# First units of a two-block transformer kernel: order of the first norm, idle products, weights in halves, gates in PSUM

## What is computed

```python
u = rmsnorm(h, norm_mix[layer])             # x * rsqrt(mean(x*x) + eps) * gain
proj = u @ w_in                             # q, f, i, g
forget = lb + (1.0 - lb) * jax.nn.sigmoid(f)
key = 1.0 - forget
log_f = jnp.log(forget)
query = jax.nn.silu(q)
# chunkwise: b = cumsum(log_f); decays exp(b_t - b_s) between query t and key s
```

## Time and profile before

| | |
|---|---|
| time, median of 3 runs | 2152.67 us (2152.38 to 2156.83) |
| the profiled execution's own time | 2158.04 us |
| its span | 2156.2 us |
| busy: PE, DVE, ACT, POOL | 2120.2, 995.1, 868.8, 1149.7 us |
| mean granted TensorE clock | 0.995 of full |

### The profile page before, as it was taken

One profiled execution on the slowest core, in us unless ns is written; L12 is line 12 of the kernel. 1 busy time (PEld: TensorE's weight loads), 2 busy tenths in 40 slices (PEclk: granted clock), 3 DMA queues, 4 the chain that ended last, 5 costly groups with the idle time before them and its releaser, 6 DMA issues. The chain is left out here.

```text
span 2156.2 us, 28081 instructions
## 1 busy us (share of the span) xinstructions
PE 2120.2 (98%) x10271; PEld 1750.4 (81%) x10271; DVE 995.1 (46%) x1562; ACT 868.8 (40%) x1250; POOL 1149.7 (53%) x642
## 2 busy tenths in 40 slices
PE   7999999999999999999999999999999999999998
PEld 6788878888888988888888888888667888888886
DVE  6666564403442057745422436563783344422433
ACT  7677653312233234434322334453764234322323
POOL 5677755545554465455554565473224555554552
PEclk9999999999999999999999999999999999999999
DMA  6122133322332322133332332322102223332332
GB/s 214 59 68 68 59 97 94 107 93 88 97 108 80 96 88 69 57 105 98 97 106 89 98 106 89 120 72 89 69 21 79 97 89 98 97 108 85 94 112 70
DMA packets 54423, 195.65 MB, mean 91 GB/s; under 512 B 6832, under 2 KB 9664, under 8 KB 53952
## 3 DMA queue, kind: packets, MB, share of 16 engines
q1 hardware_dynamic: 52864, 187.27, 27.7%
q10 hardware_dynamic: 1472, 7.19, 0.9%
HBM read 190.25 MB, written 4.19 MB: 90 GB/s over the span
## 5 line engine op out<-in xcount | busy, mean ns | idle before, releaser
L1764 POOL TENSOR_TENSOR w_split<-ring,w_split 128x1024 fp32r<-128x1024 f32 (+3 forms) x327 | 841.3, 2573 | 827.1 <-ACT w_split L1237 827.0
L1237 ACT CAST w_split<-ring 128x1024 fp32r<-128x1024 f32 (+3 forms) x327 | 356.4, 1090 | 1007.6 <-PE ps L498 876.1
L496 PE MATMUL ps<-u_split,w_split 128*128 128x512 f32 x1768 | 705.5, 399 | 10.5 <-DVE u_split L2019 9.8
L498 PE MATMUL ps<-u_split,w_split 128*128 128x512 f32 x1768 | 691.0, 391 | 0.0
L497 PE MATMUL ps<-u_split,w_split 128*128 128x512 f32 x1768 | 690.8, 391 | 0.0
L496 PEld LDWEIGHTS ps<-u_split,w_split 128*128 128x128 f32 x1768 | 333.6, 189 | 87.6 <-issue 16.9
L498 PEld LDWEIGHTS ps<-u_split,w_split 128*128 128x128 f32 x1768 | 333.2, 188 | 70.5
L497 PEld LDWEIGHTS ps<-u_split,w_split 128*128 128x128 f32 x1768 | 333.8, 189 | 69.6 <-issue 3.1
L496 PE MATMUL ps<-hid,w_split 128*128 128x512 f32 x637 | 249.0, 391 | 1.5 <-POOL hid L1959 1.4
L498 PE MATMUL ps<-hid,w_split 128*128 128x512 f32 x637 | 247.9, 389 | 0.0
L497 PE MATMUL ps<-hid,w_split 128*128 128x512 f32 x637 | 247.9, 389 | 0.0
(11 more groups left out here) (355 smaller groups left out, 2511.1 us busy)
## 6 DMA issues: line engine op xcount, KB each, us to landing
ring<-in_w_hgrn SPq DMA_DIRECT2D x32, 512.0 KB, 3.6
ring<-in_w_attn_qk SPq DMA_DIRECT2D x24, 512.0 KB, 3.5
ring<-in_w_merge SPq DMA_DIRECT2D x24, 512.0 KB, 3.3
ring<-in_w_gu0a SPq DMA_DIRECT2D x22, 512.0 KB, 3.6
ring<-in_w_gu0b SPq DMA_DIRECT2D x22, 512.0 KB, 3.5
ring<-in_w_gu1a SPq DMA_DIRECT2D x22, 512.0 KB, 3.6
ring<-in_w_gu1b SPq DMA_DIRECT2D x22, 512.0 KB, 3.5
ring<-in_w_gu2a SPq DMA_DIRECT2D x22, 512.0 KB, 3.5
```

Of the source, the lines that this page charges most:

```text
L496: nc.tensor.matmul(ps[:, bank], ws[:, 0, r, w], act[:, 0, c], start=c == 0, stop=False)
L498: m = nc.tensor.matmul(ps[:, bank], ws[:, 1, r, w], act[:, 0, c], start=False, stop=c == n - 1)
L1237: nc.scalar.copy(ws[:, 0, slot, 0:w], ring[:, r, 0:w]).then_inc(s["w_hi"], 1)
L1764: nc.gpsimd.tensor_tensor(ws[:, 1, slot, 0:w], ring[:, r, 0:w], ws[:, 0, slot, 0:w].bitcast(F32), ALU.subtract).then_inc(s["w_lo"], 1)
```

## The change

- PE first runs eight float32 matmuls of 128x512 over a tile of zeros (osq, zeroed by DVE as its first instruction) into an unused PSUM bank.
- SP loads the tile of ones behind chunk 1 of x; the semaphores of x now cover chunks 0, (1, 2), (3, 4), (5, 6), 7.
- ACT loads the Exp table first, takes the lower bounds' exponential ahead of x, and casts chunks ahead of squaring them (squares 0, 1, 2 in between, 3 behind the last cast, 4 to 7 behind the weights of unit 1). The Ln table is loaded ahead of the root.
- The eight squares are no longer added on DVE: PE sums each with a float32 matmul of its own against ones, three inside unit 0 and five inside unit 1.
- Unit 1's weights are cast on ACT in two halves and subtracted on DVE in two halves; PE starts unit 1 on the first. Unit 2's hi is copied on DVE. POOL no longer makes unit 1's lo.
- The lower bounds' maximum and differences stand ahead of the first chunk on DVE.
- For heads 0 and 1 forget is written over the sigmoid in PSUM, key is read from there, and the log is taken in place once key is done. Heads 2 to 7 (loop) still use fg.
- Some semaphores are merged (swapped, cs_norm, z_steps); no wait there changes its meaning.

The core of the diff:

```diff
@@ SP
                     for c in range(DC):
-                        sp.dma_start(h[:, c], a["x_slots"][:, c]).then_inc(s[f"x_loaded{c // 2}"], 16)
-                    sp.dma_start(ones[:], a["ones"]).then_inc(s["norm_consts"], 16)
+                        sp.dma_start(h[:, c], a["x_slots"][:, c]).then_inc(s[f"x_loaded{(c + 1) // 2}"], 16)
+                        if c == 1:
+                            sp.dma_start(ones[:], a["ones"]).then_inc(s["ones_loaded"], 16)
@@ PE
+            def first_square(c):
+
+                if c == 0:
+                    pe.wait_ge(s["ones_loaded"], 16)
+                pe.wait_ge(s["sq_ready"], c + 1)
+                m = nc.tensor.matmul(ps[:, 6], ones[:], nsq[:, c % 4], start=c == 0, stop=c == DC - 1)
+                if c < 6:
+                    m.then_inc(s["sq_sum"], 1)
+                if c == DC - 1:
+                    m.then_inc(s["ms_ready"], 1)
...
-            hgrn_project(0, 0, ready=u_chunk(0))
-            pe.wait_ge(s["norm_consts"], 16 * 3)
-            mean_square(0)
-            for k in range(1, 4):
+            pe.wait_ge(s["credit"], 1)
+            for n in range(WARM):
+                nc.tensor.matmul(ps[:, 7], osq[:, 0:P], osq, start=True, stop=True)
+            hgrn_project(0, 0, ready=beside_first({1: (0,), 3: (1,), 4: (2,)}, u_chunk(0)))
+            hgrn_project(0, 1, ready=beside_first({0: (3,), 1: (4,), 2: (5,), 3: (6,), 4: (7,)}, None), halves=True)
+            for k in range(2, 4):
                 hgrn_project(0, k)
@@ ACT, first_norm
-                nc.scalar.preload_act_table(ACT.Square)
+                nc.scalar.preload_act_table(ACT.Exp)
                 hi("hgrn", 0)
+                act.wait_ge(s["lb_steps"], 5)
+                nc.scalar.activation(lbt[:, 0:3], lbt[:, 0:3], ACT.Exp).then_inc(s["lb_steps"], 1)
                 act.wait_ge(s["norm_consts"], 16 * 2)
...
-                hi("hgrn", 1)
-                hi("hgrn", 2)
+                take_chunk(0)
+                square_chunk(0)
+                take_chunk(1)
+                take_chunk(2)
+                square_chunk(1)
+                take_chunk(3)
+                square_chunk(2)
+                for c in range(4, DC):
+                    take_chunk(c)
+                square_chunk(3)
+                act.wait_ge(w_ready[1], 16)
+                for half_w, done in ((slice(0, DC // 2 * P), "first_half_hi"), (slice(DC // 2 * P, DC * P), "w_hi")):
+                    nc.scalar.copy(ws[:, 0, 1, half_w], ring[:, 1, half_w]).then_inc(s[done], 1)
+                for c in range(4, DC):
+                    square_chunk(c)
+                nc.scalar.preload_act_table(ACT.Ln)
                 rms(0)
@@ ACT, gates
             def hgrn_log(head, dst):
+                if isinstance(head, int):
+                    act.wait_ge(s["key"], cnt(head, 1, 1))
+                    nc.scalar.activation(dst, dst, ACT.Ln).then_inc(s["log_f"], 1)
+                    return
                 act.wait_ge(s["forget"], cnt(head, 1, 1))
                 nc.scalar.activation(dst, fg, ACT.Ln).then_inc(s["log_f"], 1)
@@ POOL
-            for k in range(5):
+            for k in (0, 2, 3, 4):
                 lo("hgrn", k)
@@ DVE
-                if c >= 2:
-                    add_square(0, c - 1)
...
+            nc.vector.memset(osq, 0.0)
             nc.vector.memset(eps[:], EPS).then_inc(s["credit"], 1)
...
             for c in range(DC):
                 first_input(c)
+            first_weights()
...
-                nc.vector.tensor_scalar(fg, gate, omlb[:, col], lb[:, col], ALU.mult, ALU.add).then_inc(s["forget"], 1)
+                forget = gate if isinstance(head, int) else fg
+                nc.vector.tensor_scalar(forget, gate, omlb[:, col], lb[:, col], ALU.mult, ALU.add).then_inc(s["forget"], 1)
                 dve.wait_ge(s["forget"], cnt(head, 1, 1))
-                nc.vector.tensor_scalar(key[x], fg, -1.0, 1.0, ALU.mult, ALU.add).then_inc(s["key"], 1)
+                nc.vector.tensor_scalar(key[x], forget, -1.0, 1.0, ALU.mult, ALU.add).then_inc(s["key"], 1)
```

More of the change, by code:

```diff
@@ L484, in plain, with unit @@
                 return m
-            def unit(section, k, act, bank, i=None, per=0, n=8, ready=None, part=None):
+            def unit(section, k, act, bank, i=None, per=0, n=8, ready=None, part=None, halves=False):
                 r, v, _ = split_use(section, k, i, per)
                 lo, hi = part or (0, n)
-                if lo == 0:
+                if halves:
+                    pe.wait_ge(s["first_half_lo"], 1)
+                elif lo == 0:
                     pe.wait_ge(s["w_lo"], v)
                 for c in range(lo, hi):
+                    if halves and c == n // 2:
+                        pe.wait_ge(s["w_lo"], v)
                     if ready is not None:
@@ L595, in _, with beside_first, before, hgrn_project @@
             FREED = ("raw_f", "raw_q", "raw_g", "vf_ready")
-            def hgrn_project(head, k, ready=None, part=None):
+            def first_square(c):
[7 more added lines that the diff above has]
+                    m.then_inc(s["ms_ready"], 1)
+            def beside_first(at, ready):
+                def before(c):
+                    for n in at.get(c, ()):
+                        first_square(n)
+                    if ready is not None:
+                        ready(c)
+                return before
+            def hgrn_project(head, k, ready=None, part=None, halves=False):
                 name, first, *loop = hgrn_unit(head, k)
@@ L601, in hgrn_project @@
                     pe.wait_ge(s[FREED[k]], cnt(later(head, -1), 1, 1))
-                m = unit(name, first, us, BANK[k], *loop, ready=ready, part=part)
+                m = unit(name, first, us, BANK[k], *loop, ready=ready, part=part, halves=halves)
                 if part is None or part[1] == 8:
@@ L1418, in hgrn_log @@
             def hgrn_log(head, dst):
+                if isinstance(head, int):
+                    act.wait_ge(s["key"], cnt(head, 1, 1))
+                    nc.scalar.activation(dst, dst, ACT.Ln).then_inc(s["log_f"], 1)
+                    return
                 act.wait_ge(s["forget"], cnt(head, 1, 1))
                 nc.scalar.activation(dst, fg, ACT.Ln).then_inc(s["log_f"], 1)
[L1422 to L1423 removed]
             hgrn_sigmoid(0, "raw_f", sf_, log_bank(0), "sig_f")
+            act.wait_ge(s["w_hi"], 3)
             hi("hgrn", 3)
@@ L1595, in _ @@
             act.wait_ge(s["z_b"], 2)
-            nc.scalar.activation(zab, la, ACT.Abs).then_inc(s["z_abs"], 1)
-            act.wait_ge(s["z_abs"], 1)
-            nc.scalar.activation(zab, zab, ACT.Exp, scale=-1.0).then_inc(s["z_exp"], 1)
+            nc.scalar.activation(zab, la, ACT.Abs).then_inc(s["z_steps"], 1)
+            act.wait_ge(s["z_steps"], 1)
+            nc.scalar.activation(zab, zab, ACT.Exp, scale=-1.0).then_inc(s["z_steps"], 1)
             ahead("gla_v", 1)
-            act.wait_ge(s["z_exp"], 1)
-            nc.scalar.activation(zab, zab, ACT.Ln, bias=ones[:, 0:1]).then_inc(s["z_ln"], 1)
+            act.wait_ge(s["z_steps"], 2)
+            nc.scalar.activation(zab, zab, ACT.Ln, bias=ones[:, 0:1]).then_inc(s["z_steps"], 1)
             ahead("gla_v", 2)
@@ L2133, in _ @@
             nc.vector.memset(start[:, 2:3], 0.0).then_inc(s["o_rstd"], 2)
+            dve.wait_ge(s["norm_consts"], 16 * 2)
+            lbs = s["lb_steps"]
+            nc.vector.tensor_tensor(lbt[:, 3], lbl[:, 0], lbl[:, 1], ALU.max).then_inc(lbs, 1)
+            dve.wait_ge(lbs, 1)
+            nc.vector.tensor_tensor(lbt[:, 3], lbt[:, 3], lbl[:, 2], ALU.max).then_inc(lbs, 1)
+            dve.wait_ge(lbs, 2)
+            for r in range(3):
+                nc.vector.tensor_tensor(lbt[:, r], lbl[:, r], lbt[:, 3], ALU.subtract).then_inc(lbs, 1)
             for c in range(DC):
                 first_input(c)
+            first_weights()
             def cumulate(it, b, log_decay):
```

58 lines of the change are left out of this document (31 added, 27 removed).

## The result

| | executions | median | lowest to highest |
|---|---|---|---|
| before, first comparison | 22 | 2151.30 us | 2148.43 to 2156.83 |
| changed, first comparison | 22 | 2154.78 us | 2153.93 to 2155.47 |
| before, all comparisons | 125 | 2152.13 us | 2148.06 to 2160.70 |
| changed, all comparisons | 32 | 2154.72 us | 2153.87 to 2155.47 |

The account below looks back on a forecast made before the run. PE, busy 98% of the span, was taken as the bound. Resuming 1.25 us earlier at head 0's scores and avoiding 2.1 us of half clock gave -3.35: 2152.67 to 2149.3 us, range 2146.5 to 2153.3.

Parts of the forecast that it names:

- the stall: PE's 5.15 us wait at head 0's scores for DVE's line 2186, plus 2.1 us of half clock after it.
- The sum: At head 0's scores PE goes on at 56.95 against 58.21, 1.25 us early, without the 2.1: -3.35 us.
- Idle products: PE's start: eight products of zeros from 1.4 to 10.7 us, 1.5 later than now; unit 0's products all at 0.23.
- First input: Unit 0: no wait on input left, 0.27 + 0.30 + 0.2 us of gaps go; lower bounds may lose up to 2.4.
- Squares on PE: Units 0 and 1: six more float32 sums, 5.1 us on PE; unit 1 ends at 29.05, 2.9 us late.
- The root: Norm's root on ACT: Ln at 26.45, 5.4 us later; head 0's scan at 34.5, 3.9 us late, POOL's run likewise.
- Unit 6: Ahead of head 0's scores: POOL's weights come at 54.55, PE arrives at 53.2, waits 1.4 us, clock stays up.
- Gates in PSUM: Head 1's key on DVE takes 0.81 us instead of 9.11, so PE's wait at line 621 goes entirely.
- More of it stays: Rival: POOL's run loses only 2.9 us, quicker clock rise and zeroing: -5.1, 2147.5 us; chance 0.30 with upper tail.
- The stall moves: Rival: behind line 621, DVE's gathering or ACT's table loads make PE wait as long: -1.25, 2151.4 us; chance 0.13.
- key still waits: Rival: despite its PSUM source, head 1's key ends with POOL's run: +3.9, 2156.6 us; chance 0.05.
- zeros don't raise the clock: Rival: PE's products of zeros take 13.7 us and unit 0 still runs half speed: +3.5, 2156.2 us; chance 0.05.

Follow-up runs that it names:

- no waits at the start: unit 3 on DVE, plus unit 4's cast ahead of ACT's copy of head 0's sum, lower bounds' operations ahead of the root on DVE: 2147.76 us, again 2148.58.
- squares on DVE: Changed kernel with the squares added on DVE again and two float32 sums on PE in unit 1 in place of eight: 2150.62 us, ratio to before 0.9991.
- unit 3 on DVE: squares on DVE, plus unit 3's cast on DVE instead of ACT and POOL's subtraction for unit 6 two steps earlier: 2151.70 us, ratio 0.9998.
- key later: Kernel before with a DVE memset of 256 zeros per partition ahead of each of the first two keys: 2152.59 us, ratio 1.0005.

## Why the prediction was wrong

**What a time is made of.** For each profiled execution: its time, the date of the milestone, and what is left.

| kernel | time | milestone | rest | half clock near 1500 us |
|---|---|---|---|---|
| changed, without gates in PSUM | 2152.12 | 77.38 | 2074.74 | none |
| no waits at the start | 2145.06 | 70.31 | 2074.75 | none |
| squares on DVE | 2150.81 | 73.82 | 2076.99 | about 7 us |
| unit 3 on DVE | 2151.57 | 74.61 | 2076.96 | about 7 us |
| no idle products | 2154.29 | 77.21 | 2077.08 | about 7 us |
| before, twice | 2158.04, 2158.39 | 80.86, 81.10 | 2077.18, 2077.29 | about 7 us |
| four idle products | 2153.43 | 74.85 | 2078.58 | about 10 us |
| changed, twice | 2154.82, 2155.13 | 76.14, 76.60 | 2078.68, 2078.53 | about 10 us |
| gates in PSUM alone, twice | 2152.00, 2152.07 | 73.27, 73.58 | 2078.73, 2078.49 | about 10 us |
| key later | 2152.79 | 73.82 | 2078.97 | about 10 us |
| no waits, again | 2148.67 | 69.83 | 2078.84 | about 10 us |

The last column is worked out as above, from the granted clock in stages of 5 us, and comes to 0, 6.8 or 10.1 to 10.3 us in all 14. The edits set the milestone, and the rest has three values, 2074.7, 2077.0 to 2077.3 and 2078.5 to 2079.0, in step with that stretch. That explains all 14 profiled executions to 0.5 us. It also places the groups: before without its stall has its milestone near 73.8, which gives 2148.5, 2150.9 and 2152.3 to 2152.8; its lower 94 executions lie at 2148.06 to 2148.82 (13 of them) and 2149.1 to 2153.24, where the two upper places can't be told apart. And with the stall no time is under 80.86 + 2074.7 = 2155.6: none of the 94 can have it whole, and all 31 can.

**The sum held, and was applied to the wrong time.** The prediction put the changed kernel's profiled execution at 2154.7; it was 2154.82. That is luck in part: the milestone moved by 4.72 us instead of 3.35, and the middle gave back 1.5 where the sum had nothing. The step that failed is the last of "The sum": it saw that the profiled execution lay 5.4 us over the median of the three runs, and took the difference alone off that median. The 5.15 + 2.1 us of the stall are present in a quarter of before's executions (31 of 125). 2158.04 - 7.25 = 2150.8, which is before's lower group; so the warning was there, of the very size of the stall. Taken seriously, it says that the median already lacks the stall. Without the stall the prediction's own working has PE go on at 56.95 where it would be ready at 53.06: 3.9 us slower, 2155.2 us from the 2151.30 measured beside the change, which took 2154.78.

**What the change costs an ordinary execution.** The nearest to before without the stall is the kernel whose key comes a quarter of a microsecond later. Against it the changed kernel's second group of level scores (55.64 to 53.32) and its milestone (76.14 to 73.82) are both 2.32 us late. Against gates in PSUM alone, the helpful part of the change without the rest, the milestone is 2.87 us late (76.14 to 73.27), and the times of the two profiled executions, both with about 10 us of half clock, differ by 2.82. So the 3.9 us were 1 to 1.6 too many. Step by step:

- *Idle products*: predicted to end at 10.7. In the seven profiled executions that have eight of them they end at 9.58 (the changed kernel's), 9.74, 9.93, 9.96, 10.12 (the changed kernel's second), 10.52 and 11.01. The zeroing took 0.48 us as taken (0.5), so it is the moment of the clock's rise that differs: at 0.85 us for each at full clock, PE ran 2.6 to 5.5 us at half (an estimate from these ends), where 4.2 to 5.3 were assumed. "Longer than needed": right, by 1.1 us.
- *First input*: no wait on it in unit 0, right. DVE's first subtraction does meet POOL's, which runs from 5.61 to 7.97, and takes 2.00 us in place of 0.75, inside the 2.4 that the prediction allows; the idle products cover it.

```profile
6.52 2.00 DVE L2071 SCALAR_TENSOR_TENSOR u_split<-arena,gains_sb,u_split 128x512 fp32r<-128x512 f32 x1 [0.90 <-ACT u_split L1287]
```

- *Squares on PE*: eight sums of about 0.87 each (18.09 to the first of unit 2 at 27.93 is 9.84, of which 24 products take 24 x 0.229 = 5.5, so 4.34 for five). Right in size. PE was 1.8 us late at unit 2 where 2.9 was predicted, because unit 0 started 1.1 us sooner.
- *The root*: Ln at 25.38 against a predicted 26.45; head 0's scan 2.75 us late (30.64 to 33.39) against 3.9. POOL's run was late by the same 2.75 (33.58 to 36.33), as the prediction had it.
- *Unit 6*: its weights came at 53.47 (predicted 54.55), PE waited 1.18 (predicted 1.4), the clock stayed at 1.00 in the stage of the earlier trace rows:

```profile
50.00:60.00 10.00, 8.82 (x58) 7.80 (x57) 8.56 (x29) 8.17 (x9) 9.70 (x10) 1.00 0.18 55
```

- *Gates in PSUM*: key in 0.69 us for both heads, line 647 without a wait. Right, and the part that helps: by the whole stall in a quarter of the executions, and by head 0's hold in the others.

So the parts do what the prediction says, and the mechanism of "POOL's queue follows the root" is what makes the change slower: the runs with the sums on DVE and with four idle products give back 2.3 and 1.3 us of it at the milestone.

**The rivals.** "More of it stays" had the trace's start nearly right (-4.7 before the middle section) and the time wrong. "The stall moves", "key still waits" and "zeros don't raise the clock" are each refuted by a row above. The rival that came true was not on the list: *the stall isn't in most executions*. It gives +2.3 to +2.9 us on an ordinary execution. The prediction had given "slower" a chance of 0.06.

**What stays open.** 2.3 us from 2151.37, the median of before's lower group, make 2153.7; measured are 2154.7. The 1.0 us left is, as an estimate, the stretch at half clock. The changed kernel has the long one in both profiled executions, and none of its 32 executions lies where one without the stretch would (2150.9), while before's lower group lies in more than one of the three places. Before, the kernel without waits and the one without gates in PSUM do have executions in the low place. Why this kernel never has is not known. Nor is it known why key gets through in one execution and waits 9 us in another: shifting it by 0.27 us didn't tell.

## What to carry to other kernels

- Before a stall seen in one profiled execution is subtracted from a median, compare that execution's own time with the spread of all: if it lies above by about the price of the stall, suspect that the stall isn't in the median. A second profile doesn't help if it falls into the same group; the list of all times does.
- When PE is the bound and the helpers are dense, the first thing that each edit moves should be followed to the queue that comes next: here six sums on PE cost 2.3 us and not 5.2, by way of the root, ACT's cast and POOL's list. The gates in PSUM alone gained 0.13 and 0.17%; with the squares back on DVE and an order in which no queue is late, the idle products, halves and earlier casts brought it to 0.26 and 0.31%.

## What the runs showed of the hardware

- **A DVE operation from SBUF to SBUF can be held for a whole run of another engine's instructions, or for none.** The same 128x512 form took 9.11 and 9.12 us in the two profiles of before, ending 0.28 and 0.29 us after POOL's run of back-to-back instructions; 2.15 to 2.52 us (head 0's key, four profiles) beside a single POOL subtraction; and 0.49 and 0.70 in two others, where a POOL instruction became longer by 0.2 to 0.26 us instead. The keys of heads 2 to 7 in before, from SBUF too, took 0.43 to 1.80. With a PSUM source it took 0.69 each time, beside a POOL as busy. The Trainium skill, "SBUF — State Buffer", section "Who interferes with whom", says that whoever issues first gets the shared pair for the whole instruction and the other blocks fully. The holds of 2.15 to 2.52 us and the lengthened POOL instructions agree with it; that DVE waited through eight POOL instructions in the two long ones (46.08 to 55.31 in before), none of which is longer than 2.41 us, is more than one instruction's hold.
- **The clock can fall while PE is busy without a gap.** Around 1500 us it went to 1.2 GHz for nothing, about 7 or about 10 us, during or just behind the same 64 matmuls of 64x32, with PE at 5.00 of 5.00 us busy. The price was 0, 2.2 to 2.6 or 3.7 to 4.2 us. The Trainium skill, "TensorE: Matmul & The Clock Gate", section "What's actually happening", calls the monitor free-running and the moment of the rise at a kernel's start variable from run to run. The ends of the idle products, 9.58 to 11.01, agree with it; a fall without a gap in PE's work is more than it states.
- **A single wait of PE of 2.04 us was followed by a fall of the clock**, 1 us after it had ended. Waits of 1.14 to 1.36 us in the first 60 us were not: the granted clock was 1.00 from 28 to 68 us in the six profiles that have them.
- **Products of zeros raise the clock** as others do: the first unit's products cost 0.23 us apiece behind four or eight of them, the first ones 0.43 without.
